# A relative bias table read right side up from 128 shifted copies in device memory

## What is computed

```python
dots = jnp.einsum('bthd,bsd->bths', qib, k_idx32)          # index scores
score = ...                                                # weighted sum of relu(dots), causal
_, idx = lax.top_k(score, topk)                            # 64 keys of 256
logits = jnp.einsum('btgrd,btkgd->btgrk', qg, k_sel) * HEAD_DIM ** -0.5
dist = q_pos[None, :, None] - idx
bias = table[t5_bucket(dist)]                              # table: rel_bias, 32 buckets x 8 heads
logits = jnp.where((dist >= 0)[:, :, None, None, :], logits + bias, -jnp.inf)
p = jax.nn.softmax(logits, axis=-1)
```

## Time and profile before

| | |
|---|---|
| median of three runs | 2257.31 us |
| the profiled execution | 2254.39 us |
| its span, first to last instruction | 2252.6 us |
| mean granted clock of TensorE, share of full speed | 0.996 |
| PE busy | 98% |
| VectorE busy | 67% |
| ScalarE busy | 48% |
| POOL busy | 5% |
| moved by DMA | 474.73 MB, 211 GB/s |

### The profile page before, as it was taken

The page is one execution under the profiler, slowest core; times in us unless marked ns, Lnnn a source line. Parts: engine busy times, 40 slices in busy tenths (PEclk is TensorE's granted clock), DMA queues, the critical chain, the costliest instruction groups (busy, mean ns, idle before and its releaser), DMA issues.

```text
span 2252.6 us, 37367 instructions
## 1 busy us (share of the span) xinstructions
PE 2216.8 (98%) x15836; PEld 2065.2 (92%) x15836; DVE 1510.1 (67%) x1864; ACT 1071.6 (48%) x1422; POOL 121.5 (5%) x81
## 2 busy tenths in 40 slices
PE   7999999999999999999999999999999999999998
PEld 7889999999999888988988998998889989999986
DVE  6867588899989767554555554555766555678655
ACT  5444435554444456544443443444656545444443
POOL 1100010111100201000000000000100000011000
PEclk9999999999999999999999999999999999999999
DMA  8855667677787665656656656656754545788763
GB/s 279 240 179 163 201 211 247 218 237 254 240 267 245 236 227 178 191 196 191 196 193 195 192 194 196 201 194 204 246 173 147 157 135 165 245 295 292 254 215 139
DMA packets 246382, 474.73 MB, mean 211 GB/s; under 512 B 21054, under 2 KB 25512, under 8 KB 244424
## 3 DMA queue, kind: packets, MB, share of 16 engines
q1 hardware_dynamic: 242888, 454.40, 63.0%
q0 software_dynamic: 3328, 17.96, 2.3%
HBM read 468.09 MB, written 4.21 MB: 210 GB/s over the span
## 4 chain that ended last, share of the span: by engine, by line
PE 90%; DVE 6%; issue 1%; ACT 1%; POOL 1%; DMA 1%; POOLq 0%; SPq 0%; ACTq 0%; DVEq 0%
PE ps L867 18%; PE ps L869 18%; PE ps L868 18%; PE ps L860 11%; PE ps L862 11%; PE ps L861 11%; DVE wloW L1227 1%; DVE tmp L1255 1%; PE ps L795 1%; DVE tmp L1400 1%; PE ps L651 1%; PE ps L677 1%; ACT whiW L899 1%; POOL tmp L538 0%; PE ps L784 0%
## 5 line engine op out<-in xcount | busy, mean ns | idle before, releaser
L867 PE MATMUL ps<-op0h,whiW 128*128 128x256 f32 x3248 | 907.4, 279 | 7.7 <-DVE wloW L1227 7.7
L869 PE MATMUL ps<-op0h,wloW 128*128 128x256 f32 x3248 | 899.3, 277 | 0.0
L868 PE MATMUL ps<-op0l,whiW 128*128 128x256 f32 x3248 | 899.3, 277 | 0.0
L1227 DVE TENSOR_TENSOR wloW<-raw,whiW 128x1024 fp32r<-128x1024 f32 (+1 forms) x488 | 600.2, 1242 | 339.5 <-ACT whiW L899 337.2
L899 ACT ACTIVATE whiW<-raw 128x1024 fp32r<-128x1024 f32 (+1 forms) x488 | 512.3, 1057 | 569.6 <-PE ps L869 421.6
L867 PEld LDWEIGHTS ps<-op0h,whiW 128*128 128x128 f32 x3248 | 612.1, 188 | 11.5 <-DVE wloW L1227 7.0
L868 PEld LDWEIGHTS ps<-op0l,whiW 128*128 128x128 f32 x3248 | 612.3, 189 | 2.0 <-issue 1.4
L869 PEld LDWEIGHTS ps<-op0h,wloW 128*128 128x128 f32 x3248 | 612.2, 188 | 0.0
L1227 DVE TENSOR_TENSOR wloT<-raw,whiT 128x1024 fp32r<-128x1024 f32 (+1 forms) x280 | 338.3, 1218 | 274.3 <-ACT whiT L899 274.0
L899 ACT ACTIVATE whiT<-raw 128x1024 fp32r<-128x1024 f32 (+1 forms) x280 | 290.8, 1047 | 318.1 <-PE ps L862 257.6
L860 PE MATMUL ps<-whiT,op1h 128*128 128x512 f32 x640 | 249.4, 390 | 0.0
(11 more groups left out here) (260 smaller groups left out, 2178.1 us busy)
## 6 DMA issues: line engine op xcount, KB each, us to landing
raw<-in_w_in SPq DMA_DIRECT2D x256, 512.0 KB, 4.4
raw<-in_w_up SPq DMA_DIRECT2D x128, 512.0 KB, 3.8
raw<-in_w_down SPq DMA_DIRECT2D x128, 512.0 KB, 4.0
raw<-in_w_ada SPq DMA_DIRECT2D x96, 512.0 KB, 5.0
raw<-in_w_gate SPq DMA_DIRECT2D x96, 512.0 KB, 4.9
raw<-in_w_out SPq DMA_DIRECT2D x64, 512.0 KB, 4.4
raw<-in_w_branch SPq DMA_DIRECT2D x48, 512.0 KB, 5.2
raw<-in_w_proj_a SPq DMA_DIRECT2D x24, 512.0 KB, 5.0
```

Of the source, the lines that this page charges most:

```text
L867: pe.matmul(o, wh, xh[:, ka, :], start=first and m % 2 == 0, stop=False, skip_group_check=True)
L868: pe.matmul(o, wh, xl[:, ka, :], start=False, stop=False, skip_group_check=True)
L869: mm = pe.matmul(o, wl, xh[:, ka, :], start=False, stop=last, skip_group_check=True)
L1227: v.tensor_tensor(wlo[job.mode][q % NSPL][:, :, 0:job.n], x, h.bitcast(F32), ALU.subtract).then_inc(s_lo, 1)
```

## The change

The row is no longer stored once for each head but 128 times, each copy 513 elements behind the one before it. Reading partition p from element 127 + 512 p on then begins 127 - p elements into copy p: the row shifted the other way, which is the table as it is wanted. One read brings all eight heads straight into `bt`. The flip matrix, its load, the four turning matmuls, the four copies on ScalarE and the staging through `tmp[4]` and `tmp[5]` are gone. The read waits for the fourth `pool_weight` step, as the first of the four reads did. PE's wait for the last `index_relu` goes to the first `scores1`; VectorE's wait for the table is now one for the read. `scratch_e` grows from 12 KB to 2.1 MB.

```diff
+SKEW = 128 * 513 + 384
...
-        for i in range(4):
-            q = of["pool1"].end + 11 + 2 * i
-            side(pe_at, q, "bias_flip", i)
-            side(act_at, q + 1, "bias_flip", i)
...
             pool.wait_ge(s_erow_v, 1)
-            pool.dma_start(scratch_e, erow[0:8, :]).then_inc(s_erow_w, 16)
-            pool.dma_start(flip[:, :], a["k_flip"]).then_inc(s_flip, 16)
+
+            pool.dma_start(bass.AP(scratch_e.tensor, 0, [[SKEW, 8], [513, 128], [1, 384]]), erow[0:8, :].unsqueeze(1).broadcast_to([8, 128, 384])).then_inc(s_erow_w, 16)
             ada_sum(0)
             pool.wait_ge(s_erow_w, 16)
-            for i in range(4):
-                if i == 0:
-                    pool.wait_ge(s_pwm, 4)
-                elif i == 1:
-                    pool.wait_ge(s_plo, 4)
-                else:
-                    pool.wait_ge(s_btp, i - 1)
-                pool.dma_start(tmp[4 + i % 2][:, :].rearrange("p (h s) -> p h s", h=2),
-                               bass.AP(scratch_e.tensor, 768 * i, [[1, 128], [384, 2], [1, 256]])).then_inc(s_bt_in[i % 2], 16)
+            pool.wait_ge(s_pwm, 4)
+            pool.dma_start(bt[:, :, :], bass.AP(scratch_e.tensor, 127, [[512, 128], [SKEW, 8], [1, 256]])).then_inc(s_bt, 16)
...
-            def bias_flip(i):
-                if i == 0:
-                    pe.wait_ge(s_flip, 16)
-                    pe.wait_ge(s_idxr, 12)
-                if i >= 2:
-                    pe.wait_ge(s_bt, i - 1)
-                pe.wait_ge(s_bt_in[i % 2], 16 * (i // 2 + 1))
-                pe.matmul(bank[4 + i % 2][:, :], flip[:, :], tmp[4 + i % 2][:, :], start=True, stop=True).then_inc(s_btp, 1)
-
             def scores1(h):
                 ps = bank[4 + h % 2]
                 if h == 0:
                     pe.wait_ge(s_pair[of["q0"].pair], of["q0"].after)
                     pe.wait_ge(s_pair[of["q1"].pair], of["q1"].after)
-                if h < 2:
-                    pe.wait_ge(s_bt, 3 + h)
-                else:
+                    pe.wait_ge(s_idxr, 12)
+                if h >= 2:
                     pe.wait_ge(s_ya, h - 1)
...
-            def bias_flip(i):
-                act.wait_ge(s_btp, i + 1)
-                act.activation(bt[:, 2 * i:2 * i + 2, :], half(bank[4 + i % 2]), ACT.Copy).then_inc(s_bt, 1)
-
...
                 if h == 0:
                     v.wait_ge(s_mk, 2)
                     v.wait_ge(s_chi, 4)
-                if h < 2:
-                    v.wait_ge(s_bt, 4)
-                else:
+                    v.wait_ge(s_bt, 16)
+                    v.wait_ge(s_pwm, 4)
+                if h >= 2:
                     v.wait_ge(s_tr1, h - 1)
```

More of the change, by code:

```diff
@@ L55, in constants @@
     cd = np.concatenate([np.cos(b), -np.sin(b)], 1) / math.sqrt(256 * 128)
-    f = {"k_ident": np.eye(128), "k_flip": np.eye(128)[::-1], "k_pm": pm, "k_onehot": onehot, "k_cm": cm, "k_rc": rc, "k_rs": rs,
+    f = {"k_ident": np.eye(128), "k_pm": pm, "k_onehot": onehot, "k_cm": cm, "k_rc": rc, "k_rs": rs,
          "k_cs": cs, "k_cd": cd}
@@ L353, in program @@
         oneh = bg("oneh", [128, 384], 70)
-        flip = bg("flip", [128, 128], 70)
         vst = bg("vst", [128, 128], 71.5)
@@ L424, in program @@
         s_turn, s_turned, s_oper = sem("x_turned"), sem("x_scaled"), sem("x_operand")
-        s_erow, s_erow_v, s_erow_w, s_flip, s_bt_in = sem("bias_row"), sem("bias_row_read"), sem("bias_row_stored"), sem("flip"), [sem("bias_in0"), sem("bias_in1")]
-        s_btp, s_bt = sem("bias_flipped"), sem("bias_table")
+        s_erow, s_erow_v, s_erow_w, s_bt = sem("bias_row"), sem("bias_row_read"), sem("bias_row_stored"), sem("bias_table")
         s_idx, s_idxr, s_idxs, s_mk = sem("index_dots"), sem("index_relu"), sem("index_sum"), sem("mask")
@@ L819, in _ @@
             parts = {"turn_x": turn_x, "vectors_b": vectors_b, "bias_row": bias_row, "index_dots": index_dots, "pool_window": pool_window, "pool_weight": pool_weight,
-                     "bias_flip": bias_flip, "scores1": scores1, "turn1": turn1, "values1": values1, "turn_x": turn_x,
+                     "scores1": scores1, "turn1": turn1, "values1": values1, "turn_x": turn_x,
                      "turn_qk": turn_qk, "scores2": scores2, "turn2": turn2, "values2": values2, "fourier_t": fourier_t, "fourier_d": fourier_d}
@@ L1029, in _ @@
             parts = {"vectors_b": vectors_b, "ctx_square": ctx_square, "x1_square": x1_square, "x2_square": x2_square, "turn_x": turn_x, "index_relu": index_relu,
-                     "pool_window": pool_window, "pool_scale": pool_scale, "bias_flip": bias_flip, "softmax1_exp": softmax1_exp,
+                     "pool_window": pool_window, "pool_scale": pool_scale, "softmax1_exp": softmax1_exp,
                      "turn1": turn1, "values1": values1, "scale_qk": scale_qk, "turn_qk": turn_qk, "softmax2_exp": softmax2_exp, "turn2": turn2,
@@ L1720 @@
     out = nc.dram_tensor("out_dram", (1, 256, D), F32, kind="ExternalOutput").ap()
-    se = nc.dram_tensor("scratch_e", (8, 384), F32).ap()
+    se = nc.dram_tensor("scratch_e", (8, SKEW), F32).ap()
     sx = nc.dram_tensor("scratch_x", (256, D), F32).ap()
```

## The result

The changed kernel takes 2273.35 us (median of 4 runs, 2270.06 to 2276.09), the kernel before beside it 2257.94 us (4 runs, 2256.19 to 2259.6). The ratio is 1.007, with a 95% interval from 1.0055 to 1.0085: slower by 15.4 us, where 3 us less was forecast and 2262.5 us was the upper end of the range. The profiled execution took 2273.76 us with a span of 2271.9 us, 19.3 us more than the span before.

What follows compares the result with a forecast made beforehand. PE, busy 98% of the span, was taken as the bound. Profiled: 2254.39 - 3.48 + 0.49 + 0 (store) = 2251.4 us; against the median, 2257.31 - 3.0 = 2254.3 us, range 2252.5 to 2262.5.

Steps and rivals of the forecast that it cites:

- What goes away on PE: At the four turning steps, their matmuls leave PE's queue: 0.87 us per step, 3.5 us in all.
- what VectorE takes back: Near 220 us, PE arrives before VectorE's low part is ready and waits 0.5 us, leaving 3.0 us gained.
- The wait put at 219.90 us: PE, arriving at 219.90, waits about 0.5 us for the low part that VectorE ends at 220.39.
- The reads, POOL's order, the moved waits: At about 188 us, one 1 MB read takes 12 us under 155 us of cover; nothing is held, no cost.
- The length of the store: From 44.13 us, 1.57 MB needs 6.2 us of the DMA engines, or 12.4 us if only half work.
- the estimate of 29 us: Store from 44 us at 54 GB/s by the skill's port rule, holding the engines until about 73 us.
- What the store does to the weight loads: Loads beside the store from 44 us: between 0 and 12.4 us of cost, taken as 0.
- The burst of the earlier trace: Just before 780 us, X and g1b loads: weight loads took 11.1 instead of 4.4 us, yet PE stayed busy.
- The cover: From 44 to 72 us, 28 us to drain the store's backlog before ScalarE's DMA waits, 22.2 us in 14.
- the rival: Store holds weight loads from 44 to 91 us, deciding if still standing at 72.5: 6.7 us, 2261.0 us; chance 0.27.
- the tight stage: Behind 72 us, ScalarE waits for DMA and PE idles 2.66 us at 94.66; unrecovered load time adds one for one.
- The other rivals: VectorE or later PE waits take the gain back, 2257.3 us, chance 0.13; waits at 94.66 and 396 shrink, 2252, chance 0.1.

Runs made afterwards that it cites:

- the one-copy run: Changed kernel storing the row once, 12 KB, with the single read adapted and the table left upside down; ratio 0.9987, 2252.75 against 2254.67 us.
- the 16-copy version: Changed kernel with 16 shifted copies instead of 128 and eight reads instead of one, table right; 2252.54 against 2255.55 us, ratio 0.9985.
- the run with the store alone: Kernel before plus the large store from partitions 0 to 7 of x0 into memory nobody reads, nothing else changed; 2277.3 us, ratio 1.0098.

## Why the prediction was wrong

**What goes away on PE**: right. 4 x 0.87 us less what VectorE takes back, 0.5 us, was to be 3.0 us or 0.13%; the one-copy run has 0.13%, the 16-copy version 0.15%, each give or take 0.09%, so the match to a hundredth is luck and the sign is not. The wait put at 219.90 us with 0.49 us appeared with 0.41 us. That result rested on the start times in the earlier trace rows and on low parts followed one by one.

**The reads, POOL's order, the moved waits**: right. The read took 6.5 us instead of the 12 allowed, and nothing waited for it.

**The length of the store**: wrong, and the first of two failed steps. The prediction took it from the store of X, which leaves 128 partitions, as 6.2 us, or 12.4 us if half the engines work; it was 34.7. That half the engines would work was right, as the share of 48.2% shows. Wrong was the pace given to each of them, that of the store of X: from 44 to 79 us the store's queue held engines for 42.3% x 16 x 35 us = 237 us, where 12.4 us on eight engines are 99. The number of partitions does not set that pace: eight partitions four apart land in 14.5 us, eight neighbours in 34.4. What counts is how many groups of four neighbours the source has: two give 45 GB/s, four give 86. In the prediction's text this stood as the estimate of 29 us from the Trainium skill (SBUF — State Buffer, "Door 1: The DMA port swizzle", 27 GB/s for such a group, and partitions 0 to 7 on two of them). The runs bear the rule out for reading from SBUF, at 21.6 to 22.7 GB/s beside the weight loads. It got a chance of 0.27, although it was the only statement at hand about this very shape, and the rows only spoke of others.

**What the store does to the weight loads**: wrong, the second failed step. The sum has 0 for this term; PE's two waits between 44 and 90 us alone are 15.9 us. The burst of the earlier trace rows was read as "twice as large, and it cost nothing". But that burst ran at 409 GB/s, with the engines full of moving data; it made loads 2.5 times as long. The slow store left 80 GB/s for everything, and loads of 3.2 us took up to 29.8. A share of 0.82 says that the engines had time to spare, not that a slow source would let it be used: on the engines of the store each weight packet had to wait 0.70 us for its turn.

**The cover**: from the earlier trace rows the prediction took 22.2 us as all of ScalarE's waits for data in the first 120 us, but that row is for whiT alone; whiW has 4.7 us more in three, two of them at 26 and 29 us. This changes nothing here. What failed is the length of the cover: the prediction gave the backlog until 72 us, 28 us from the issue, to be worked off. The true cover is what PE has prepared plus the few loads that get through: it ran dry after 16.8 us. In the kernel before with the store added, 10.0 us of store cost nothing, 18.2 us cost about 6. So the rival had its place and its mechanism right and its point of decision wrong. Its price, 6.7 us as loads beside a burst show, was too small for the same reason as the step above; even its upper bound, 2266.7 us, lies below 2270. The price should have been the store's length less the cover, with the clock and the tight stage on top: 34.7 - 16.8 = 17.9, where the two waits in that stage are 15.9 us, with one chunk worked in between at the lower clock, and the whole front of the kernel came out 23.9 us late.

**The other rivals**: VectorE's waits later in the kernel moved with PE, as the argument against that rival had it. That for L1389, now L1363, is 3.0 us as before; that for wloW from 390 to 600 us is 1.1 us instead of 0.3, but it is 1.1 us as well in the run with the store alone, which has all its matmuls.

## What to carry to other kernels

Count a transfer's time by its source and destination partitions before its bytes: a repeated read out of a few neighbouring partitions was slow here, and every weight load in flight paid for it. Compare a new transfer with a row of the same shape; if the trace has none, and a documented rule speaks of that very shape, give its outcome more weight than rows about other shapes; here it was the better guide. The price of a stalled loader is about the length of the stall less the prepared work, and the lower clock after it; a shorter store (16 copies) that fits into the cover has the same gain for nothing. And when an experiment changes the size of the pieces, read in the trace what size the packets had.

## What the runs showed of the hardware

- Reading from SBUF, four neighbouring partitions together gave 22.7 GB/s (8 partitions, 34.7 us) and 21.6 GB/s (16 partitions, 18.2 us) for 1.57 MB. Eight partitions four apart gave 1.57 MB / 14.5 us = 108 GB/s, almost what 128 partitions gave beside the same loads (13.5 us, 116 GB/s).
- A slow transfer from one queue held the loads of another queue: from 52 to 60 us all DMA moved 61 GB/s with the store out of eight neighbours, against 171 and then 304 with the same bytes from 128 partitions.
- The two queues took turns by packets: 44 packets of the store and 44 of the weight loads in 4 us, at 0.70 us for one of the store. Pieces of 1,536 and of 512 bytes both travelled in packets of some 4 KB (4.5 and 4.2), and the smaller pieces made the store 38.4 us, no better.
- Destination rows every 2,052 bytes and every 2,048 bytes took the same: 34.4 and 34.3 us.
- After PE had stood still for 6.82 and 9.05 us, its granted clock was at the lower of its two levels, 1.2 of 2.4 GHz, for part of what followed: 0.50 of full speed from 65 to 70 us, 0.66 on average from 60 to 85 us.
